# Gate/up weights laid four rows to a partition, and loaded 4 MB at a time straight into their slots from expert 18 on

## The chip, the cores and the metric

One core of one Trainium2 chip runs the whole kernel in one launch. The metric is the device time of that launch in microseconds (us). Its engines are TensorE (PE in the profile, PEld its weight loads), VectorE (DVE), ScalarE (ACT), GpSimd (POOL) and SyncE (SP), which here only waits and starts transfers; 16 DMA engines carry the transfers.

## What is computed

Two transformer blocks on 256 tokens of width 1024, all in fp32. The first is a mixing layer (stick-breaking attention and gated linear attention) with a convolutional feed-forward layer, the second pooling and latent attention with a mixture of 32 experts. The change touches the experts. Each token goes to its best 4 of 32 experts; an expert multiplies its tokens by a 1024x2048 matrix (gate and up, 8 MB) and by a 1024x1024 matrix (down, 4 MB):

```python
def expert_block(args):
    xblk, e = args
    gu = xblk @ w_gate_up[e] + b_gate_up[e]
    gate = jnp.minimum(gu[:, :D_EXPERT], SWIGLU_LIMIT)
    up = jnp.clip(gu[:, D_EXPERT:], -SWIGLU_LIMIT, SWIGLU_LIMIT)
    act = gate * jax.nn.sigmoid(SWIGLU_ALPHA * gate) * (up + 1)
    return act @ w_down[e] + b_down[e]
```

With these inputs 31 experts have at most 64 tokens, and expert 8 has 72.

## The kernel before

The first block and the attention of the second take about the first 480 us of the span. What follows is the experts, in order, as **jobs** of up to 64 tokens (`SLOTS`): one job for each expert, and a second one on the same weights for expert 8, so 33 jobs. A job is, on TensorE: `gate_up` for pairs 0 to 3 (L2432), a gather of the next job's tokens (L2428, `gather`, for the first jobs also L2415), four transposes of the activations (L2470), a bias, and `down` (L2535). The parts of the former job's result are added in between (L2492, L2502), and the job of expert 29 also makes the bias of the down matrices (L2515, `late=True`). The last job is written out apart (`last_turn`), and takes its pairs 1, 2 and 3 in halves (L2457).

**Weights.** An expert's 12 MB fill 12 slots of 8 KB in each partition: 8 for gate/up (`GU`), 4 for down (`DN`). Two neighbouring slots are a *pair* or *part* of 2 MB, and are loaded by one transfer: parts 0 to 3 are gate/up, 4 and 5 are down (`PARTS = 6`). In each partition a part takes 16 KB that are contiguous in memory, two rows of the matrix. Slots 0 to 5 are in `ring`, 6 to 11 in `ring_b`. The gather must pick the same rows of the model's width for its operand: `k_rows` steps by 2.

**Two ways into the slots.** SyncE starts all the loads, in the order of experts and parts.

- *Staged*, experts 1 to 25 (`STAGED = 26`; parts 0 and 1 of expert 1 go straight): a part goes to one of four places of 2 MB (`stage`, `stage_b`), and GpSimd copies it from there into its slots in four copies (`put_in_place`, L653), once TensorE has used what stands there. A place is filled again when its part has been copied (L422).
- *Straight*, experts 26 to 31: `next_part` waits until TensorE has used the part of the expert before (`part_used`) and loads the next one over it (L419). For expert 31, parts 1, 2, 3 and 5 come in two halves of 1 MB each (L486), with 8 KB in each partition.

TensorE waits for `in_place[part]`, which the last copy of GpSimd or the transfer itself raises. A part of an expert with two jobs is free after its second job. `gu_used` counts gate/up slots that TensorE is done with, `gu_full` is raised with the last of them, `d_used` counts down slots.

Of the kernel before, what the change touches and what calls it, by code (L numbers as in the profile page):

```python
# [32 lines left out]
P = 128  # L33
# [3 lines left out]
KT = D // P  # L37
# [13 lines left out]
E, TOPK, FE = 32, 4, 1024  # L51
# [6 lines left out]
RING = 6  # L58
CW = 2048
GU, DN = 8, 4  # L60
PAIRS = GU // 2
PARTS = PAIRS + DN // 2
PLACES = 4
STAGED = E - 6
SPLIT = 28
HI = 3

# [225 lines left out]
    return n % RING, 16 * (n // RING + 1)  # L293


def job_slot(g, slot):

    return g.t.ring[:, slot, :] if slot < RING else g.t.ring_b[:, slot - RING, :]


def pair_slot(g, pair):


    n, ring = (2 * pair, g.t.ring) if 2 * pair < RING else (2 * pair - RING, g.t.ring_b)
    return ring[:, n:n + 2, :].rearrange("p c n -> p (c n)")


def stage_place(g, place):
# [20 lines left out]
def part_used(g, job, part):  # L329

    return half_used(g, job, part, 1)
# [27 lines left out]
def sync_program(g, sp):  # L359
# [49 lines left out]
    sp.wait_ge(s.ff_o, FF_STEPS - 2)  # L409
    load_ffn(FF_STEPS - 1, "o", 0, FF_STEPS - 1)  # L410

    gate_up = w["w_gate_up_2"].rearrange("e (c p i) n -> e c p (i n)", p=P, i=2)
    down = w["w_down_2"].rearrange("e (h p i) n -> e h p (i n)", h=2, p=P)

    def part(e, k):
        return gate_up[e, k] if k < PAIRS else down[e, k - PAIRS]

    def load_part(e, k):
        sp.dma_start(pair_slot(g, k), part(e, k)).then_inc(s.in_place[k], 16)  # L419
# [19 lines left out]
        sp.dma_start(t.bias_raw[32 * q:32 * q + 32, :],  # L439
                     w["b_gate_up_2"][:, FE * (q // 2):FE * (q // 2) + FE]).then_inc(s.bias_in, 16)  # L440
    sp.dma_start(t.b_down[0:E, :], w["b_down_2"]).then_inc(s.b_down_in, 16)
    load_part(0, 3)
    load_part(0, 5)
    sp.wait_ge(*g.r2.filled("pp11"))
    load_part(0, 1)
# [1 line left out]
    load_stage(1, 3, 1)  # L447
    sp.wait_ge(s.msq_ready, NORM_AT["mla"] + 1)
    sp.wait_ge(*g.r2.filled("pa11"))
    load_part(0, 2)  # L450
    load_part(0, 4)
    load_stage(1, 4, 2)
    load_stage(1, 5, 3)
# [21 lines left out]
                load_stage(m * 2 + (q + 2), k, staged_at(q, k)[0])  # L475
    with sp.Fori(STAGED - 1, E - 2) as m:
        last = last_job(m)
        for k in range(PARTS):
            next_part(m + 1, last, k)
    last = last_job(E - 2)  # L480
    for k in range(PARTS):
# [29 lines left out]
def gpsimd_program(g, pool):  # L511
# [133 lines left out]
    def put_in_place(last, k, place, landed):  # L645

        pool.wait_ge(s.staged[place], landed)
        for i in range(2):
            pool.wait_ge(*half_used(g, last, k, i))
            pool.sem_inc(s.turn_begun, 1)  # L650
            for q in (2 * i, 2 * i + 1):
                cols = slice(D * q, D * q + D)
                ins = pool.tensor_copy(pair_slot(g, k)[:, cols], stage_place(g, place)[:, cols])  # L653
        ins.then_inc(s.in_place[k], 16)
# [4 lines left out]
    with pool.Fori(0, (STAGED - 2) // 2) as m:  # L659
        for q in range(2):  # L660
            last = last_job(m * 2 + (q + 1))
            for k in range(PARTS):
                place, landed = staged_at(q, k)
                put_in_place(last, k, place, m * 48 + 16 * landed)

    rsqrt("end2")

# [2 lines left out]
def scalar_program(g, act):  # L670
# [6 lines left out]
    def square(name, sem, value, b=0, scratch=None):  # L677
# [5 lines left out]

    act.preload_act_table_set("natural_log_exp_and_others")
    load_vectors(g, act, t.vec_b, VEC_B, s.vec_b_in)
    act.dma_start(t.vec_c[0:PAIRS, :], w["vectors"]["ffn_norm"].rearrange("a (k n) -> (a k) n", k=PAIRS)).then_inc(
        s.vec_b_in, 16)
    square("mix", s.x_in[0], 16)
    act.dma_start(t.pos_i[:], w["positions"].rearrange("(b p) -> p b", p=P),
# [352 lines left out]
def vector_program(g, dve):  # L1042
# [68 lines left out]
    for h in range(2):  # L1111
        for b in range(NB):
# [5 lines left out]
                          ALU.subtract).then_inc(s.x_split, 1)  # L1118
    split_lo(1)
    bank, done = out_of(r1, "vecb")  # L1120
    step(dve.tensor_copy(t.gain_x[:].rearrange("p (c i) -> p i c", i=2),
                         bank[:, P:P + KT].rearrange("p (i c) -> p i c", i=2)))
    dve.tensor_copy(t.vec_T[:, ROWS_A:], bank[:, 0:ROWS_B]).then_inc(done, 1)
    split_lo(2)
    split_lo(3)
# [680 lines left out]
def tensor_program(g, pe):  # L1806
# [63 lines left out]
            turn_quarter(r1, "xT", t.x_n, b, h)  # L1870
    pe.wait_ge(s.vec_b_in, 16 * (len(VEC_B) + 1))
    bank = open_bank(r1, "vecb")
    for i in range(2):
        pe.transpose(bank[:, P + PAIRS * i:P + PAIRS * i + PAIRS], t.vec_c[0:PAIRS, i:2 * P:2],
                     t.ident[0:PAIRS, 0:PAIRS])
    pe.transpose(bank[:, 0:ROWS_B], t.vec_b[0:ROWS_B, :], t.ident[0:ROWS_B, 0:ROWS_B]).then_inc(s.filled, 1)

    WHOLE = ((0, 0), (0, 1), (0, 2), (1, 0), (1, 1), (1, 2))
# [530 lines left out]
    def gather_one(f0, n):  # L2409


        for f in range(f0, f0 + n):
            k_rows = slice(2 * P * (f // 2) + f % 2, 2 * P * (f // 2) + 2 * P, 2)
            for b in range(NB):
                ins = pe.matmul(banks[6][:, (f - f0) * SLOTS:(f - f0 + 1) * SLOTS], t.h_n[:, b, k_rows],  # L2415
                                t.picks[:, b, 0:SLOTS], start=(b == 0), stop=(b == 1))
        ins.then_inc(s.gathered, 1)

    def gather(m, o):


        pe.wait_ge(s.picked, nth(m, o, 4, 2))
        pe.wait_ge(s.half_ready, nth(m, o, 1, 0))
        pe.wait_ge(s.x_parted, nth(m, o, 1, 0))
        for f in range(KT // 2):
            k_rows = slice(2 * P * (f // 2) + f % 2, 2 * P * (f // 2) + 2 * P, 2)
            for b in range(NB):
                ins = pe.matmul(banks[6][:, f * P:(f + 1) * P], t.h_half[:, b, k_rows], t.picks[:, b, :],  # L2428
                                start=(b == 0), stop=(b == 1))
        ins.then_inc(s.gathered, 1)  # L2430
# [214 lines left out]
class Semaphores:  # L2645
    def __init__(self, new):
# [136 lines left out]
class Buffers:  # L2783
# [41 lines left out]
    def vectors(self, new):  # L2825

        self.vec_a = new("vec_a", [P])
        self.vec_b = new("vec_b", [P])
        self.vec_c = new("vec_c", [2 * P])

    def mixer(self, new):

# [192 lines left out]
```

## Time and profile before

| | |
|---|---|
| median of 3 runs | 1412.66 us (1411.87 to 1412.95) |
| the profiled execution, its own time | 1416.75 us |
| its span | 1415.0 us |
| TensorE busy | 1364.8 us (96%) |
| GpSimd busy | 727.1 us (51%) |
| bytes moved | 480.81 MB, mean 340 GB/s |
| transfers from 540 us to the end of the experts | 428 GB/s but for one dip |

The span is what the profile sees; the execution's own time is 1.75 us longer, and both stand some 2 to 4 us above the median of the runs without a profile. A matmul's end is modelled, so TensorE shows as busy while it is partly waiting; waits are read from the gaps that the timeline prints in brackets, with what ended them. Each transfer's packets are shared by the 16 DMA engines.

### The profile page before, as it was taken

What the parts mean: (1) busy time and instruction counts of PE and PEld (TensorE: products, weight loads), DVE (VectorE), ACT (ScalarE), POOL (GpSimd) and SP (SyncE); (2) the same over time, 40 slices, a digit from 0 to 9 for tenths busy, and PEclk for the clock granted to TensorE, in tenths of its full rate; (3) what the DMA queues carried; (4) which work ended last, traced back from release to release, by engine and by line L of the source; (5) the groups of instructions that cost most, each with busy time, mean ns of one, the idle gap of its engine ahead of it and who ended that gap; (6) DMA issues with size and microseconds to landing.
All of it is one profiled execution on the core that took longest, in us unless ns stands there. A gap on an engine that the chain in (4) does not pass through costs nothing.

```text
span 1415.0 us, 21682 instructions
## 1 busy us (share of the span) xinstructions
PE 1364.8 (96%) x7692; PEld 778.8 (55%) x7693; DVE 754.7 (53%) x1157; ACT 304.4 (22%) x461; POOL 727.1 (51%) x723
## 2 busy tenths in 40 slices
PE   8999999999999999999999999999989999999997
PEld 8899989999976744434434334334333343334332
DVE  7675788877656546444455545444444444433322
ACT  5645453344316200000000101001000010001001
POOL 3000023322144069888869888888888888600000
PEclk9999999999999999999999999999999999999999
DMA  9444355555556889999999999999999999999996
GB/s 320 158 145 146 119 179 179 178 178 179 183 211 237 340 337 428 429 429 428 426 403 425 428 428 427 428 428 428 427 428 428 429 427 427 428 429 427 427 424 263
DMA packets 78284, 480.81 MB, mean 340 GB/s; under 512 B 7116, under 2 KB 31369, under 8 KB 53161
## 3 DMA queue, kind: packets, MB, share of 16 engines
q1 hardware_dynamic: 74910, 477.71, 83.2%
q10 hardware_dynamic: 3338, 2.62, 0.6%
q8 instruction: 24, 0.39, 0.1%
q14 instruction: 12, 0.09, 0.0%
HBM read 479.26 MB, written 1.05 MB: 339 GB/s over the span
## 4 chain that ended last, share of the span: by engine, by line
PE 54%; DMA 22%; issue 15%; POOL 5%; DVE 2%; ACT 1%; POOLq 0%; SPq 0%; DVEq 0%; ACTq 0%
DMA stage<-in_w_gate_up 14%; PE bank L2442 13%; DMA stage<-in_w_down 7%; PE bank L2130 7%; PE bank L1900 6%; PE bank L2550 6%; PE bank L2158 4%; POOL ring_b L653 3%; POOL ring L653 2%; PE bank L1850 2%; PE bank L2057 2%; PE bank L2095 2%; PE bank L1916 2%; PE bank L2428 1%; PE bank L2492 1%
## 5 line engine op out<-in xcount | busy, mean ns | idle before, releaser
L2442 PE MATMUL bank<-ring,x_T 128*64 128x512 f32 x1552 | 351.0, 598 | 22.9 <-POOL ring L653 16.8
L653 POOL COPY ring_b<-stage 128x1024 f32<-128x1024 f32 x252 | 266.8, 1102 | 45.0 <-DMA stage<-in_w_down 21.9
L2442 PEld LDWEIGHTS bank<-ring,x_T 128*64 128x64 f32 x1552 | 106.7, 137 | 246.3 <-issue 196.8
L2550 PE MATMUL bank<-ring_b,act_T 128*64 128x512 f32 x1056 | 233.9, 595 | 0.5 <-ACT act_T L999 0.5
L653 POOL COPY ring<-stage 128x1024 f32<-128x1024 f32 x192 | 198.4, 1078 | 36.7 <-DMA stage<-in_w_gate_up 24.9
L1707 DVE TENSOR_TENSOR h<-h,bank 128x512 f32<-128x512 f32 x124 | 79.6, 684 | 190.4 <-PE bank L2492 190.4
L2550 PEld LDWEIGHTS bank<-ring_b,act_T 128*64 128x64 f32 x1056 | 72.9, 137 | 144.3 <-issue 129.4
L532 POOL TENSOR_TENSOR rstd<-msq,neg_half 128x2 f32<-128x2 f32 (+2 forms) x9 | 7.7, 859 | 271.7 <-DVE msq L1066 218.0
L1683 DVE SCALAR_TENSOR_TENSOR y_lo<-bank,slot_gate,y_hi 128x512 fp32r<-128x512 f32 x33 | 24.8, 751 | 207.3 <-ACT y_hi L979 207.3
L573 POOL TENSOR_TENSOR ff_lo<-ring,ff_hi 128x2048 fp32r<-128x2048 f32 x11 | 53.0, 4820 | 145.2 <-PE bank L2130 96.5
L993 ACT ACTIVATE sig<-bias_raw 128x512 f32<-128x512 f32 x33 | 20.8, 629 | 490.8 <-DVE bias_raw L1718 490.8
L2442 PE MATMUL bank<-ring_b,x_T 128*64 128x512 f32 x512 | 116.9, 598 | 7.0 <-POOL ring_b L653 5.2
L653 POOL COPY ring<-stage_b 128x1024 f32<-128x1024 f32 x100 | 102.5, 1068 | 40.0 <-PE bank L2442 27.7
L2130 PE MATMUL bank<-h_hi,ff_hi 128*128 128x256 f32 x320 | 90.6, 283 | 0.0
L2130 PE MATMUL bank<-h_hi,ff_lo 128*128 128x256 f32 x320 | 90.6, 283 | 0.0
L2130 PE MATMUL bank<-h_lo,ff_hi 128*128 128x256 f32 x320 | 90.5, 283 | 0.0
L1101 DVE TENSOR_TENSOR ring_r<-ring,w_hi 128x2048 fp32r<-128x2048 f32 x28 | 64.1, 2295 | 27.2 <-ACT w_hi L709 27.1
L2442 PEld LDWEIGHTS bank<-ring_b,x_T 128*64 128x64 f32 x512 | 33.9, 136 | 74.4 <-issue 62.1
L979 ACT ACTIVATE y_hi<-bank,slot_gate 128x512 fp32r<-128x512 f32 x33 | 22.7, 687 | 231.9 <-PE bank L2550 231.9
L2428 PE MATMUL bank<-picks,h_half 128*128 128x128 f32 x512 | 68.1, 286 | 0.0
L858 ACT ACTIVATE ff_hi<-ring 128x2048 fp32r<-128x2048 f32 x33 | 61.6, 1905 | 28.5 <-DMA ring<-in_w_ffn_in 25.5
L2428 PEld LDWEIGHTS bank<-picks,h_half 128*128 128x128 f32 x512 | 62.8, 196 | 0.8 <-issue 0.8
(491 smaller groups left out, 2129.4 us busy)
## 6 DMA issues: line engine op xcount, KB each, us to landing
stage<-in_w_gate_up SPq DMA_DIRECT2D x73, 2048.0 KB, 15.0
stage<-in_w_down SPq DMA_DIRECT2D x38, 2048.0 KB, 15.1
stage_b<-in_w_gate_up SPq DMA_DIRECT2D x25, 2048.0 KB, 15.2
ring<-in_w_gate_up SPq DMA_DIRECT2D x21, 2048.0 KB, 23.8
ring_b<-in_w_down SPq DMA_DIRECT2D x13, 2048.0 KB, 23.0
stage_b<-in_w_down SPq DMA_DIRECT2D x12, 2048.0 KB, 15.2
ring<-in_w_in SPq DMA_DIRECT2D x22, 1024.0 KB, 5.6
ring<-in_w_ffn_in SPq DMA_DIRECT2D x22, 1024.0 KB, 6.0
```

The source lines that it names most:

```text
L573: pool.tensor_tensor(t.ff_lo[:, 1, :], t.ring[:, slot, :], t.ff_hi[:, slot, :].bitcast(F32), ALU.subtract).then_inc(s.ff_lo_pool, 1)
L653: ins = pool.tensor_copy(pair_slot(g, k)[:, cols], stage_place(g, place)[:, cols])
L858: act.activation(t.ff_hi[:, n % RING, :], t.ring[:, n % RING, :], ACT.Copy).then_inc(s.ff_hi_done, 1)
L1101: dve.tensor_tensor(t.ring_r[:, n % RING, :], t.ring[:, n % RING, :], t.w_hi[:, n % HI, :].bitcast(F32), ALU.subtract).then_inc(s.w_split, 1)
L1707: dve.tensor_tensor(t.h[:, b, cols], t.h[:, b, cols], g.banks[2 + c][:], ALU.add).then_inc(s.added, 1)
L1850: ins = pe.matmul(bank[:, 0:n], src[:, k, b * P:(b + 1) * P], wk[:, c0:c0 + n], start=(k == 0), stop=(k == len(weights) - 1))
L1900: ins = pe.matmul(into[f // 2][:, (f % 2) * T:(f % 2 + 1) * T], wt[:, k, f * P:(f + 1) * P], xt[:, 4 * half + k, :], start=((half, part) = ...
L2130: ins = pe.matmul(bank[:, f * T:(f + 1) * T], wt[:, k, f * P:(f + 1) * P], ht[:, k, :], start=(k == 0 and part == 0), stop=(k == KT - 1 an ...
L2158: ins = pe.matmul(banks[2 * b + c][:], ut[:, q, k, b * P:(b + 1) * P], wt[:, k, 512 * c:512 * c + 512], start=False, stop=last, skip_group ...
L2428: ins = pe.matmul(banks[6][:, f * P:(f + 1) * P], t.h_half[:, b, k_rows], t.picks[:, b, :], start=(b == 0), stop=(b == 1))
L2442: ins = pe.matmul(banks[n][rows, :], t.x_T[:, c, :], job_slot(g, c)[:, c0:c0 + 512], start=False, stop=(c == GU - 1), skip_group_check=True)
L2550: ins = pe.matmul(banks[4][rows, :], t.act_T[:, k, SLOTS * (c // 2):SLOTS * (c // 2) + SLOTS], job_slot(g, GU + c)[:, c0:c0 + 512], start= ...
```

## The change

Three things change together.

1. The gate/up matrix is laid out with **four** rows to a partition. Four neighbouring slots, a *quad* (4 MB), are then 32 KB of contiguous memory in each partition. A part of 2 MB is the one or the other half of that, so its 16 KB in each partition stand 32 KB apart in memory. The gather's `k_rows` steps by 4, and the gain vector `gain_x` is put in the same order (four small transposes of `vec_c` in place of two).
2. From expert 18 on (`STAGED = 18`) nothing is staged. For experts 18 to 30, `load_quad` loads parts 0 and 1 by one transfer of 4 MB, and parts 2 and 3 by another; each starts when TensorE has used both parts. Down's parts are as before. Expert 31 is loaded as before.
3. A quad raises `quad_in`; GpSimd waits for it and raises the two `in_place` that TensorE waits for. So that a quad is one piece, slots 4 to 7 are now in `ring_b`, and down's first pair is in `ring`. Of expert 0, the parts 2 and 3 change places in the order of loading.

```diff
-STAGED = E - 6
+STAGED = E - 14
...
-    n, ring = (2 * pair, g.t.ring) if 2 * pair < RING else (2 * pair - RING, g.t.ring_b)
+    ring, n = slot_home(g, 2 * pair)
...
-    gate_up = w["w_gate_up_2"].rearrange("e (c p i) n -> e c p (i n)", p=P, i=2)
+    gate_up = w["w_gate_up_2"].rearrange("e (c p i) n -> e c p (i n)", p=P, i=4)
...
     def part(e, k):
-        return gate_up[e, k] if k < PAIRS else down[e, k - PAIRS]
+        if k >= PAIRS:
+            return down[e, k - PAIRS]
+        half = 2 * CW * (k % 2)
+        return gate_up[e, k // 2][:, half:half + 2 * CW]
+
+    def load_quad(e, quad):
+        sp.dma_start(quad_slot(g, quad), gate_up[e, quad]).then_inc(s.quad_in[quad], 16)
...
     with sp.Fori(STAGED - 1, E - 2) as m:
         last = last_job(m)
-        for k in range(PARTS):
+        for quad in range(2):
+            sp.wait_ge(*part_used(g, last, 2 * quad + 1))
+            load_quad(m + 1, quad)
+        for k in range(PAIRS, PARTS):
             next_part(m + 1, last, k)
...
+    with pool.Fori(0, E - 1 - STAGED) as m:
+        for quad in range(2):
+            pool.wait_ge(s.quad_in[quad], m * 16 + 16)
+            pool.sem_inc(s.turn_begun, 1)
+            for pair in (2 * quad, 2 * quad + 1):
+                pool.sem_inc(s.in_place[pair], 16)
...
-            k_rows = slice(2 * P * (f // 2) + f % 2, 2 * P * (f // 2) + 2 * P, 2)
+            k_rows = slice(4 * P * (f // 4) + f % 4, 4 * P * (f // 4) + 4 * P, 4)
```

What SyncE has in a row in its loop over straight experts, before: a wait and a transfer of 2 MB (128x4096 fp32) for each of the four gate/up parts (down's two follow).

```order
L461 ISA
L419 ISA [waits gu_used]
L419 DMA ring<-in_w_gate_up 128x4096
L461 REGISTER_ALU
L419 ISA [waits gu_used]
L419 DMA ring<-in_w_gate_up 128x4096
L461 REGISTER_ALU
L419 ISA [waits gu_used]
L419 DMA ring<-in_w_gate_up 128x4096
L461 ISA
L419 ISA [waits gu_full]
L419 DMA ring_b<-in_w_gate_up 128x4096
```

The same place now:

```order
L500 ISA
L437 ISA [waits gu_used]
L437 DMA ring<-in_w_gate_up 128x8192
L500 ISA
L437 ISA [waits gu_full]
L437 DMA ring_b<-in_w_gate_up 128x8192
```

Two waits and two transfers are gone; the first transfer now waits for part 1 where part 0 was loaded as soon as part 0 was used, and the second for part 3.

What GpSimd has behind its staged loop, before: nothing but the last norm.

```order
L653 COPY ring_b<-stage 128x1024 [waits d_used]
L653 COPY ring_b<-stage 128x1024
L659 REGISTER_ALU
L659 COMPARE_AND_BRANCH
L532 TENSOR_TENSOR rstd<-msq,neg_half 128x2 [waits msq_ready]
```

And now (`sem_inc` prints no row of its own):

```order
L677 COPY ring_b<-stage 128x1024 [waits d_used]
L677 COPY ring_b<-stage 128x1024
L683 REGISTER_ALU
L683 COMPARE_AND_BRANCH
L689 UNCONDITIONAL_BRANCH
L689 ISA
L689 REGISTER_ALU [waits quad_in0,quad_in1]
L689 COMPARE_AND_BRANCH
L556 TENSOR_TENSOR rstd<-msq,neg_half 128x2 [waits msq_ready]
```

A loop of 13 turns has come in, which waits for each quad and passes the signal on. The staged loop above it has 8 turns in place of 12.

## Rows read from the trace of the kernel before

**Rows 1.** The page: GB/s in 40 slices of 35.4 us.

```profile
GB/s 320 158 145 146 119 179 179 178 178 179 183 211 237 340 337 428 429 429 428 426 403 425 428 428 427 428 428 428 427 428 428 429 427 427 428 429 427 427 424 263
```

**Rows 2.** Windows (busy us of each engine, then PEclk, DMA share, GB/s).

```profile
540.00:570.00 30.00, 30.00 (x160) 12.73 (x160) 18.82 (x26) 3.08 (x8) 26.78 (x26) 1.00 1.01 428
...
720.00:750.00 30.00, 30.00 (x157) 12.30 (x154) 16.04 (x24) 3.16 (x8) 19.30 (x19) 1.00 0.96 394
...
1110.00:1140.00 30.00, 27.38 (x140) 10.66 (x138) 13.23 (x21) 2.42 (x6) 25.56 (x25) 1.00 1.01 428
...
1240.00:1370.00 130.00, 122.54 (x614) 48.94 (x614) 45.54 (x100) 11.42 (x29) 0.00 (x0) 1.00 1.01 428
```

**Rows 3.** Timeline of SyncE and GpSimd around 740 us (start, us, what).

```profile
735.60 7.96 POOL L653 COPY ring<-stage 128x1024 f32<-128x1024 f32 x8 [8.91 <-PE bank L2442]
...
739.75 4.29 SPq L422 DMA_DIRECT2D stage<-in_w_down  x2
```

**Rows 4.** Timeline of TensorE, job of expert 29 (start, us, line, brackets: idle before and its end).

```profile
1316.65 3.65 PE L2442 MATMUL bank<-ring,x_T 128*64 128x512 f32 x16 [0.20 <-DMA ring<-in_w_gate_up]
...
1323.10 3.65 PE L2442 MATMUL bank<-ring,x_T 128*64 128x512 f32 x16 [0.88 <-DMA ring<-in_w_gate_up]
...
1328.40 3.65 PE L2442 MATMUL bank<-ring,x_T 128*64 128x512 f32 x16
...
1333.70 3.65 PE L2442 MATMUL bank<-ring_b,x_T 128*64 128x512 f32 x16
```

**Rows 5.** Timeline of TensorE, one row of the job of expert 28, then those of 30 and 31.

```profile
1292.16 3.65 PE L2442 MATMUL bank<-ring,x_T 128*64 128x512 f32 x16 [1.24 <-DMA ring<-in_w_gate_up]
...
1348.03 3.60 PE L2442 MATMUL bank<-ring,x_T 128*64 128x512 f32 x16
...
1352.48 3.65 PE L2442 MATMUL bank<-ring,x_T 128*64 128x512 f32 x16 [0.85 <-DMA ring<-in_w_gate_up]
...
1357.37 3.65 PE L2442 MATMUL bank<-ring,x_T 128*64 128x512 f32 x16 [0.59 <-DMA ring<-in_w_gate_up]
...
1362.27 3.65 PE L2442 MATMUL bank<-ring_b,x_T 128*64 128x512 f32 x16 [0.58 <-DMA ring_b<-in_w_gate_up]
...
1366.50 2.13 PE L2428 MATMUL bank<-picks,h_half 128*128 128x128 f32 x16
...
1369.69 7.09 PE L2550 MATMUL bank<-ring_b,act_T 128*64 128x512 f32 x32
...
1385.44 3.65 PE L2457 MATMUL bank<-ring,x_T 128*64 128x512 f32 x16
...
1389.69 1.94 PE L2457 MATMUL bank<-ring_b,x_T 128*64 128x512 f32 x8
...
1391.88 1.94 PE L2457 MATMUL bank<-ring_b,x_T 128*64 128x512 f32 x8 [0.25 <-DMA ring_b<-in_w_gate_up]
...
1393.75 0.44 PE L2479 MATMUL bank<-ident,mix_in 128*128 128x128 f32 x2
```

**Rows 6.** Timeline of SyncE: issues of the loads of expert 31.

```profile
1351.67 0.34 SPq L419 DMA_DIRECT2D ring<-in_w_gate_up  x1
...
1365.97 0.80 SPq L486 DMA_DIRECT2D ring_b<-in_w_gate_up  x2
```

**Rows 7.** Lines L2428 and L2470 (duration in ns: min/median/max).

```profile
L2428 PEld LDWEIGHTS bank<-picks,h_half x512: 194/196/198, 511.9 to 1368.2; 128*128 128x128 f32 x171
...
L2428 PE MATMUL bank<-picks,h_half x512: 281/281/385, 511.9 to 1368.3; 128*128 128x128 f32 x171
...
L2470 PEld LDWEIGHTS bank<-ident,act x132: 196/208/220, 514.3 to 1396.3; 128*128 128x128 f32 x132
...
L2470 PE MATMUL bank<-ident,act x132: 272/283/387, 514.3 to 1396.4; 128*128 128x128 f32 x132
```

**Rows 8.** The chain that ended last: a landing, and what precedes the next copy by GpSimd.

```profile
973.11 15.21 DMA stage<-in_w_down
989.84 0.69 issue
```

More of the change, by code:

```diff
@@ L293, in slot_use, with slot_home, quad_slot @@
     return n % RING, 16 * (n // RING + 1)
+def slot_home(g, slot):
+    if slot < 4 or slot in (GU, GU + 1):
+        return g.t.ring, slot if slot < 4 else slot - 4
+    return g.t.ring_b, slot - 4 if slot < GU else slot - 6
 def job_slot(g, slot):
-    return g.t.ring[:, slot, :] if slot < RING else g.t.ring_b[:, slot - RING, :]
+    ring, n = slot_home(g, slot)
+    return ring[:, n, :]
 def pair_slot(g, pair):
-    n, ring = (2 * pair, g.t.ring) if 2 * pair < RING else (2 * pair - RING, g.t.ring_b)
+    ring, n = slot_home(g, 2 * pair)
     return ring[:, n:n + 2, :].rearrange("p c n -> p (c n)")
+def quad_slot(g, quad):
+    return (g.t.ring if quad == 0 else g.t.ring_b)[:, 0:4, :].rearrange("p c n -> p (c n)")
 def stage_place(g, place):
@@ L441, in sync_program @@
     sp.dma_start(t.b_down[0:E, :], w["b_down_2"]).then_inc(s.b_down_in, 16)
-    load_part(0, 3)
+    load_part(0, 2)
     load_part(0, 5)
@@ L449, in sync_program @@
     sp.wait_ge(*g.r2.filled("pa11"))
-    load_part(0, 2)
+    load_part(0, 3)
     load_part(0, 4)
@@ L685, in scalar_program @@
     load_vectors(g, act, t.vec_b, VEC_B, s.vec_b_in)
-    act.dma_start(t.vec_c[0:PAIRS, :], w["vectors"]["ffn_norm"].rearrange("a (k n) -> (a k) n", k=PAIRS)).then_inc(
+    act.dma_start(t.vec_c[0:2, :], w["vectors"]["ffn_norm"].rearrange("a (k n) -> (a k) n", k=2)).then_inc(
         s.vec_b_in, 16)
@@ L1120, in vector_program @@
     bank, done = out_of(r1, "vecb")
-    step(dve.tensor_copy(t.gain_x[:].rearrange("p (c i) -> p i c", i=2),
-                         bank[:, P:P + KT].rearrange("p (i c) -> p i c", i=2)))
+    step(dve.tensor_copy(t.gain_x[:].rearrange("p (c i) -> p i c", i=4),
+                         bank[:, P:P + KT].rearrange("p (i c) -> p i c", i=4)))
     dve.tensor_copy(t.vec_T[:, ROWS_A:], bank[:, 0:ROWS_B]).then_inc(done, 1)
@@ L1872, in tensor_program @@
     bank = open_bank(r1, "vecb")
-    for i in range(2):
-        pe.transpose(bank[:, P + PAIRS * i:P + PAIRS * i + PAIRS], t.vec_c[0:PAIRS, i:2 * P:2],
-                     t.ident[0:PAIRS, 0:PAIRS])
+    for i in range(4):
+        pe.transpose(bank[:, P + 2 * i:P + 2 * i + 2], t.vec_c[0:2, i:4 * P:4], t.ident[0:2, 0:2])
     pe.transpose(bank[:, 0:ROWS_B], t.vec_b[0:ROWS_B, :], t.ident[0:ROWS_B, 0:ROWS_B]).then_inc(s.filled, 1)
@@ L2425, in gather @@
         for f in range(KT // 2):
-            k_rows = slice(2 * P * (f // 2) + f % 2, 2 * P * (f // 2) + 2 * P, 2)
+            k_rows = slice(4 * P * (f // 4) + f % 4, 4 * P * (f // 4) + 4 * P, 4)
             for b in range(NB):
@@ L2773, in __init__ @@
         self.half_in = {(k, i): new(f"half_in{k}{i}") for k in HALVED for i in range(2)}
+        self.quad_in = [new(f"quad_in{n}") for n in range(2)]
         self.in_place = [new(f"in_place{n}") for n in range(PARTS)]
@@ L2828, in vectors @@
         self.vec_b = new("vec_b", [P])
-        self.vec_c = new("vec_c", [2 * P])
+        new("under_sb_s", [12928])
+        self.vec_c = new("vec_c", [4 * P])
     def mixer(self, new):
```

## The prediction

> **What bounds the kernel now.** I read the page's row of GB/s first: from slice 16 on (566 us) nearly every slice stands at 427 to 429 GB/s, to the one before the last [rows 1]. So the transfers set the end of the experts. The exception is slice 20, with 403. The windows give the rest [rows 2]. At 540:570 TensorE is busy for 30.00 of 30 us and GB/s are at 428 as well; at 720:750 only at 394; later TensorE is idle (27.38 of 30 us at 1110:1140) and the transfers stay at 428, staged or straight (1240:1370).
>
> So there are three stretches. *Up to about 740 us TensorE leads.* It began with two experts' weights at hand, and expert 8's second job needs no new ones; the four places are full and the transfers run dry. GpSimd was idle for 8.91 us until TensorE had used a slot, began to copy at 735.60, and SyncE could start the next transfer at 739.75 [rows 3]. Whatever TensorE loses before this moves all that follows. *From there to 1392 us the transfers lead.* TensorE takes parts 1, 2 and 3 of expert 30 at 1352.48, 1357.37 and 1362.27, each after a wait for its transfer [rows 5]: 4.90 us to a part of 2 MB, 29.4 us to an expert, and nothing but a faster transfer shortens it. Part 1 of expert 28 was taken at 1292.16 and that of 29 at 1323.10, so there is also one slip of 1.5 us (30.94 against 29.38) [rows 4, 5]. *At the end TensorE and the transfers are close:* in the job of expert 31 it waits for part 3's second half for only 0.25 us [rows 5], and then a chain without weights follows.
>
> **The change, part by part.** The sum is made against the profiled execution (1416.75 us, span 1415.0) as a difference, and this is then put on the median, 1412.66.
>
> *Staging gone for experts 18 to 25.* Nothing, by itself: 428 GB/s staged and straight [rows 2]. GpSimd's copies go, but TensorE waits for transfers there. When SyncE turns from places to slots it needs work ahead. The first quad starts when two parts of expert 17 are used, at most 4 us for a part's copy and 7.9 us of matmuls after the first landed; the other five parts are 24.5 us of transfers, so about 12 us of them are still to come. I see no bubble.
>
> *The job with quads.* TensorE now starts pairs 0 and 1 when all 4 MB have landed, so where part 1 landed before, and pair 2 where part 3 landed. From part 3's place to the end of `down` and back it must fit in before the next quad. From [rows 5]: a pair and its combine 4.25 (1385.44 to 1389.69), pair 3 up to `down` 7.42 (1362.27 to 1369.69), `down` 7.0. Together 18.7 us, where the next expert's first quad lands 19.6 us later (four parts of 4.90). It fits, with 0.9 us to spare. Pairs 0 and 1 take 7.9 of the 9.8 us between quads. Each slot is then used up to 4.2 us later than before; what SyncE starts for expert 31, at 1351.67 (part 0) and 1365.97 (part 3) [rows 6], is taken 25 us after its start and more, so 4 us less leave the queue full. The job of expert 29, with its down bias, is longer: pair 0 and first bias 5.57 (1316.65 to 1323.10 less the wait of 0.88), then 5.30, 5.30, and 14.33 from pair 3 to the next job [rows 4, 5], 30.5 us in all. It starts expert 30 at 1353.6, 1.1 us late, and 7.9 us later, at 1361.5, TensorE is in time for part 3's place at 1362.27. So up to there the transfers still lead, and nothing is lost.
>
> *The last jobs: +3.8 us.* This is the main term. The delay has nothing behind which to hide at the end, as expert 31 needs TensorE's whole job after that of 30. Before, pair 3 of expert 30 began at 1362.27. Now pair 2 does. Then: pair 2 and combine 4.25, pair 3 up to `down` 7.42, from `down` to pair 2 of expert 31 15.75 (1369.69 to 1385.44), pair 2 and combine 4.25, pair 3 3.6. Sum 35.3: 1397.5, where pair 3 was done at 1393.75 before [rows 5]. That is +3.8. What follows is the same chain, and down's parts land no later than before.
>
> *GpSimd's hop: +0.2 us.* A quad's landing reaches TensorE through GpSimd. Below: nothing (TensorE waited on the transfer itself). Above: 0.69 us, the row between a landing and GpSimd's next copy [rows 8], which holds more instructions. It counts once, in front of the last two jobs.
>
> *Longer rows: -2.0 us.* No transfer with 32 KB to a partition is in the trace. The nearest rows are expert 31's halves, with 8 KB to a partition. From part 3 of expert 30 (1362.27) to the second half of part 3 of expert 31 (1391.88) it takes 29.61 us, with three parts in halves, and 29.38 without [rows 5]: 0.077 us for each part cut in two. A quad is two parts joined: 26 quads give 2.0 us. Between 0 (if rows are cut at 16 KB anyway) and twice it.
>
> *The gather's step of 4: +1.2 us before 740 us, +0.1 in the last jobs.* Up to the dip, 9 gathers of 16 matmuls and 48 more at the start use the strided operand, 192 in all. With step 2 a weight load takes 196 ns and a matmul 281 ns. The transposes of `act` have step 4, and 208 and 283 ns [rows 7]. The loads lie under matmuls in part, so 2 to 12 ns for each, 0.4 to 2.3 us; I take 6 ns, as a 128x128 load is about as long as the work it lies under. The Trainium skill (SBUF — State Buffer, section on the DMA port swizzle) says that SBUF lines are 16 bytes, full rate needs two hits per line, and a step of four fp32 values is where it ends. By that rule every element is now a line of its own, which speaks against the change; the 12 ns agree in sign, and if the loads doubled from 196 ns it would be up to 38 us over the 192.
>
> *Staged halves of 32 KB rows: 0.* Experts 2 to 17 now read 16 KB and skip 16 KB. Expert 31's halves read 8 and skip 8, and lost only the 0.077 us above. The bounds are -5 and +5 us (1% of the 450 us in which such parts move).
>
> *The rest: 0.* The order of parts 2 and 3 of expert 0, two more small transposes at the start.
>
> Sum: 3.8 + 0.2 - 2.0 + 1.2 + 0.1 = **+3.3 us**: 1416.0 for the median, 1420 for a profiled execution.
>
> **The rivals.** A change of 0.2% is 2.8 us, about what a measurement of this kernel can tell from none.
>
> 1. *Rows are cut at 16 KB*: no gain from quads, +5.3 us, 1418. For it: no longer row is shown. Against it: 8 KB and 16 KB differ as whole rows would.
> 2. *The joined rows save twice as much*, 4 us: +1.3, 1414. For it: a transfer fewer as well as rows fewer. Against: the halves had both, too.
> 3. *The staged reads with gaps are slower by 1%*: +4.5 on top, 1420.5. Against: the halves.
> 4. *The clock.* TensorE's longest regular wait is 1.24 us now [rows 5] with a granted clock of 1.00 [rows 2], its 2.4 GHz. In front of pair 2 the wait becomes 1.9 us. If the clock then falls to its lower level, 1.2 GHz, the next pair takes 7.2 us in place of 3.6: +3.6 in the last jobs, 1419.5. In earlier jobs it would eat its own cause.
> 5. *The other side, faster.* The quads move faster than the halves let expect. To pay for 5.3 us and another 2.8, each of 26 must save 0.31 us of its 9.79, four times my value, and the transfers would run at 442 GB/s. Then 1409 or less. Nothing in the rows speaks for it. The Trainium skill (same page, section on the DMA setup-cost knee) would: about 2 us fixed for each transfer, so make each as large as can be; by it 26 transfers fewer would save up to 52 us. Here parts follow each other every 4.90 us, with the next one under way, so the fixed part is hidden; where the queue is full I give the rule little.
>
> **How the numbers follow.** The forecast has 0.52; its own range is +1.0 to +5.0, as the gather, the hop and the slip of 1.5 us may fall, and I put 0.32 of it over +2.8 and 0.20 under. Rival 1 has 0.13, rival 2 0.14, rival 3 0.08, rival 4 0.06, rival 5 0.07. Slower: 0.32 + 0.13 + 0.08 + 0.06 = 0.59; the same: 0.20 + 0.14 = 0.34; faster 0.07. The range goes from 1411.5 (rival 2 with a free gather and no slip) to 1420.5 (rival 3), which leaves out rival 5 and the ends of 3 and 4.
>
> **What would show it.** In the profile after: parts of expert 31 and quads taken in a rhythm of 9.7 us, not 9.8; pair 2 of expert 30 starting with a wait of 0.7 to 1.9 us on GpSimd's signal or the quad; pair 3 of expert 31 without any wait, ending 35.3 us after pair 2 of expert 30 began; L2428's successor with a longer weight load; the dip at 740 us about 1 us later. The forecast is wrong if TensorE still waits for part 3 of expert 31, if a slice at 428 falls, or if the experts' transfers run dry near 990 us.

## The result: 1449.3 us against 1412.8, 2.5% slower

The changed kernel took 1449.3 us (median of 4 runs, 1447.09 to 1451.24), the kernel before beside it 1412.81 us (1411.87 to 1416.81). The ratio is 1.025 with an interval of 1.0236 to 1.0264: 36.5 us more, where the forecast was 3.3 more and the range ended at 1420.5. The prediction was wrong, in size and in place. One execution of experiment 3, at 1721.62 us and a mean granted clock of 0.75, where its others have 0.997 or 0.998, is left out of that experiment's ratio.

The page of the changed kernel: its span, TensorE's and GpSimd's busy time, and GB/s in 40 slices of 36.2 us.

```profile
span 1448.0 us, 21340 instructions
...
PE 1422.9 (98%) x7694; PEld 843.9 (58%) x7695; DVE 730.2 (50%) x1157; ACT 304.4 (21%) x461; POOL 522.0 (36%) x531
...
GB/s 314 174 147 125 135 190 156 198 195 165 217 150 309 276 317 429 428 428 429 428 280 372 430 428 428 429 428 383 405 427 429 429 437 427 430 428 435 426 423 201
```

The spans differ by 33.0 us and not by 36.5, because the profiled execution of the kernel before was itself 4 us above its median. TensorE is busy for 58 us more than it was. The row of GB/s has two holes: 280 and 372 from 724 to 796 us, where before there was the one slice of 403 near 740 [rows 1], and 383 and 405 from 977 us on, where before there was none. Everywhere else from slice 16 to the one before the last they stand at 423 or more. So nothing is wrong with the transfers' rate. They stood still twice, and what let them stand still is to be looked for on TensorE.

The lines of the gather (L2457, before L2428) and of the transposes of `act` (L2499, before L2470), as in [rows 7]: duration in ns, min/median/max.

```profile
L2457 PEld LDWEIGHTS bank<-picks,h_half x512: 309/330/332, 518.6 to 1401.5; 128*128 128x128 f32 x171
L2457 PE MATMUL bank<-picks,h_half x512: 396/397/500, 518.6 to 1401.6; 128*128 128x128 f32 x171
...
L2499 PEld LDWEIGHTS bank<-ident,act x132: 194/208/302, 522.2 to 1429.2; 128*128 128x128 f32 x132
L2499 PE MATMUL bank<-ident,act x132: 272/283/387, 522.4 to 1429.4; 128*128 128x128 f32 x132
```

A weight load of the gather takes 330 ns where it took 196, a matmul 397 where it took 281. The transposes, with the same step of 4, stand at 208 and 283 as ever. The timeline of TensorE shows what this is in time that nobody else can use:

```profile
546.65 3.97 PE L2457 MATMUL bank<-picks,h_half 128*128 128x128 f32 x16
550.46 0.63 PE L2499 MATMUL bank<-ident,act 128*128 128x128 f32 x4
```

Sixteen matmuls now hold the engine for 3.81 us (546.65 to 550.46). Before, the row of 2.13 us [rows 5] was followed by the transposes after 1.96 us:

```profile
1366.50 2.13 PE L2428 MATMUL bank<-picks,h_half 128*128 128x128 f32 x16
1368.46 0.63 PE L2470 MATMUL bank<-ident,act 128*128 128x128 f32 x4
```

That is 1.85 us more for each gather, 0.116 us for each matmul, where the sum of the prediction had 0.006. Every job does a gather, and up to the first hole TensorE leads.

The first hole, GpSimd and SyncE of the changed kernel, as in [rows 3]:

```profile
757.03 8.05 POOL L677 COPY ring<-stage 128x1024 f32<-128x1024 f32 x8 [23.24 <-PE bank L2471]
...
761.29 4.29 SPq L443 DMA_DIRECT2D stage<-in_w_down  x2
```

GpSimd waits 23.24 us for TensorE (before 8.91) and begins to copy at 757.03 (before 735.60). The dip is 21.4 us later, not "about 1". It accounts for 21.4 of the 33.0 us. The other 11.6 us come after it, and here are the windows of that stretch (columns as in [rows 2]) and TensorE's waits for a quad in all of it:

```profile
960.00:1020.00 60.00, 60.00 (x290) 26.06 (x288) 22.18 (x44) 4.84 (x12) 47.02 (x46) 1.00 0.91 384
...
1140.00:1200.00 60.00, 60.00 (x290) 26.23 (x291) 19.74 (x46) 5.50 (x14) 0.00 (x0) 1.00 1.00 428
1200.00:1260.00 60.00, 58.01 (x280) 25.45 (x278) 18.16 (x42) 4.84 (x12) 0.00 (x0) 1.00 1.00 429
```

```profile
PE bank L2471 <- POOLq L694: 5.3, 5, 1.1
```

TensorE is never idle up to 1200 us. Before, it was waiting for transfers already at 1110:1140 (27.38 of 30 us) [rows 2]. Then five waits for quads follow, 5.3 us together, the first of them ending at 1212.40. So what bounds the kernel has changed from 760 to about 1210 us: there TensorE with its longer job leads, and the transfers set the pace only for the last experts.

### The profile page after: what moved, and what is told of

Same layout as the page of the kernel before. It is cut to its first block, busy times and chain, and to the rows that moved or that the text cites. A ratio compares the mean times of both kernels' runs of the same rounds, so it can differ in the third digit from the quotient of the medians.

```text
span 1448.0 us, 21340 instructions
## 1 busy us (share of the span) xinstructions
PE 1422.9 (98%) x7694; PEld 843.9 (58%) x7695; DVE 730.2 (50%) x1157; ACT 304.4 (21%) x461; POOL 522.0 (36%) x531
## 4 chain that ended last, share of the span: by engine, by line
PE 84%; DMA 9%; issue 4%; DVE 2%; ACT 0%; POOLq 0%; SPq 0%; DVEq 0%
PE bank L2471 28%; PE bank L2579 12%; DMA ring_b<-in_w_gate_up 9%; PE bank L2159 7%; PE bank L2457 7%; PE bank L1929 6%; PE bank L2187 4%; PE bank L2521 3%; PE bank L1880 2%; PE bank L2086 2%; PE bank L2124 2%; PE bank L1945 2%; PE bank L2292 1%; PE bank L2245 1%; PE bank L2499 1%
## 5 line engine op out<-in xcount | busy, mean ns | idle before, releaser
L2471 PE MATMUL bank<-ring_b,x_T 128*64 128x512 f32 x1024 | 235.2, 602 | 5.3 <-POOLq L694 5.3
L2471 PE MATMUL bank<-ring,x_T 128*64 128x512 f32 x1040 | 232.3, 599 | 0.0
L677 POOL COPY ring_b<-stage 128x1024 f32<-128x1024 f32 x168 | 179.8, 1112 | 21.7 <-DMA stage<-in_w_gate_up 9.0
L677 POOL COPY ring<-stage 128x1024 f32<-128x1024 f32 x132 | 132.4, 1047 | 51.2 <-PE bank L2471 25.0
L2457 PE MATMUL bank<-picks,h_half 128*128 128x128 f32 x512 | 127.2, 402 | 0.0
L2457 PEld LDWEIGHTS bank<-picks,h_half 128*128 128x128 f32 x512 | 121.9, 329 | 0.8 <-issue 0.8
L2579 PE MATMUL bank<-ring,act_T 128*64 128x512 f32 x528 | 120.6, 599 | 0.5 <-ACT act_T L1029 0.5
L2579 PE MATMUL bank<-ring_b,act_T 128*64 128x512 f32 x528 | 118.9, 592 | 0.0
L2579 PEld LDWEIGHTS bank<-ring_b,act_T 128*64 128x64 f32 x528 | 38.0, 137 | 75.3 <-issue 75.3
L2579 PEld LDWEIGHTS bank<-ring,act_T 128*64 128x64 f32 x528 | 35.0, 137 | 68.8 <-issue 56.9
```

The costliest lines, as they stand in the source:

```text
L2471: ins = pe.matmul(banks[n][rows, :], t.x_T[:, c, :], job_slot(g, c)[:, c0:c0 + 512], start=False, stop=(c == GU - 1), skip_group_check=True)
L2579: ins = pe.matmul(banks[4][rows, :], t.act_T[:, k, SLOTS * (c // 2):SLOTS * (c // 2) + SLOTS], job_slot(g, GU + c)[:, c0:c0 + 512], start= ...
```

## The experiments

**1. The gather's step alone.** The kernel before, with one thing changed:

```diff
-k_rows = slice(2 * P * (f // 2) + f % 2, 2 * P * (f // 2) + 2 * P, 2)
+k_rows = slice(4 * P * (f // 4) + f % 4, 4 * P * (f // 4) + 4 * P, 4)
```

> The kernel before with one edit: the gather's operand is read with a step of 4 instead of 2 (it then picks other rows than the reference, the work is the same). Theory A, the step itself doubles a gather's matmul from 118 to 235 ns: about 21.4 us more up to the dip near 740 us, as in the changed kernel (735.60 against 757.03), then the transfers lead at 29.4 us to an expert against a job of 28.05, and the last gather adds 1.9: about 1436 us, and the dip with GpSimd's long wait at about 757. Theory B, the quads and the early end of the staging cost the most: within 5 us of 1413. Theory C, the reads with gaps in memory are what is slow: 1413.

Measured: 1442.98 us against 1413.8, ratio 1.0206 (1.019 to 1.0222), 29.2 us more. No transfer was touched, and the time is most of the way to the changed kernel's. Its gather, its hole and its transfers late in the kernel:

```profile
L2428 PEld LDWEIGHTS bank<-picks,h_half x512: 308/330/332, 517.7 to 1395.0; 128*128 128x128 f32 x171
```

```profile
756.18 4.10 POOL L653 COPY ring<-stage 128x1024 f32<-128x1024 f32 x4 [23.24 <-PE bank L2442]
```

```profile
1260.00:1320.00 60.00, 60.00 (x290) 26.14 (x288) 20.25 (x51) 4.85 (x12) 0.00 (x0) 1.00 1.01 428
```

The step of four, alone, makes the same weight load and the same wait of 23.24 us. My expectation of 1436 was some 7 us short. I had let the transfers take the lead again after the hole, but TensorE is busy for 60.00 of 60 us at 1260:1320 and waits for no transfer after 760 us. At 428 GB/s an expert takes 29.4 us and a job of TensorE now takes 28.05 (its gathers start at 1163.82 and 1191.87 in the changed kernel), so the transfers gain only on TensorE's stock, 1.35 us a job, and the experts run out first.

**2. The rest alone.** The changed kernel with the gather's step back at 2, on layout, staging and quads as changed:

```diff
-k_rows = slice(4 * P * (f // 4) + f % 4, 4 * P * (f // 4) + 4 * P, 4)
+k_rows = slice(2 * P * (f // 2) + f % 2, 2 * P * (f // 2) + 2 * P, 2)
```

> The changed kernel with one edit: the gather's step is 2 again (it then picks rows that do not match the layout of the weights). Theory A: only the rest of the forecast is left, +3.8 for the last jobs, +0.2 for the hop, -2.0 for the longer rows: about 1414.9 us, between 1412.5 and 1418. Theory B: 1430 or more. Theory C: some part of the 36 us stays, a rate below 425 GB/s in the staged stretch.

Measured: 1415.42 us (11 runs), ratio 1.0015 (1.0006 to 1.0025), by the ratio 2.1 us more than before. The forecast without its terms for the gather was +2.0. Its last jobs, as in [rows 5]:

```profile
1357.13 3.65 PE L2471 MATMUL bank<-ring_b,x_T 128*64 128x512 f32 x16 [1.54 <-POOLq L694]
...
1365.60 2.13 PE L2457 MATMUL bank<-picks,h_half 128*128 128x128 f32 x16
...
1388.80 3.65 PE L2486 MATMUL bank<-ring_b,x_T 128*64 128x512 f32 x16
1392.38 0.44 PE L2508 MATMUL bank<-ident,mix_in 128*128 128x128 f32 x2
```

Pair 2 of expert 30 starts after a wait of 1.54 us, pair 3 of expert 31 starts with none, and it is done 35.25 us after pair 2 began (1357.13 to 1392.38); the prediction had 35.3. From the end of pair 3 of expert 31 back, this part stands as it was forecast. Only the distance can be compared and not the place: GpSimd's copies after the first hole began at 732.58 in this execution and at 735.60 in the one of the kernel before.

The trace also shows rival 4 at work. At 1297.26 TensorE comes out of a wait of 1.97 us, and its pair takes 5.32 us in place of 3.65:

```profile
1297.26 5.32 PE L2471 MATMUL bank<-ring_b,x_T 128*64 128x512 f32 x16 [1.97 <-POOLq L694]
```

```profile
1295.30:1297.26 1.96, 0.00 (x1) 0.00 (x1) 1.29 (x2) 0.00 (x0) 0.00 (x0) 0.99 0.94 401
1297.26:1300.60 3.34, 3.34 (x8) 0.99 (x10) 0.00 (x0) 0.00 (x0) 0.00 (x0) 0.50 1.00 427
1300.60:1304.00 3.40, 3.40 (x18) 1.06 (x16) 0.72 (x2) 0.00 (x0) 0.00 (x0) 0.99 1.02 434
```

The granted clock is 0.50, the lower level of 1.2 GHz, for 3.3 us behind the wait, and 0.99 again after that. Such falls stand behind five of the seven waits of 1.96 to 1.98 us in this trace (at 1034.21, 1121.89, 1180.35, 1238.82 and 1297.26). Behind the other two, at 1004.97 and 1092.66, the pair took its 3.65:

```profile
1004.97 3.65 PE L2471 MATMUL bank<-ring_b,x_T 128*64 128x512 f32 x16 [1.96 <-POOLq L694]
```

A fall costs 1.7 us there and nothing in the end: from 1034.21 to 1297.26 these pairs start every 29.23 us whether the clock fell or not, since TensorE waits for the next quads anyway. After the 1.54 us at 1357.13, the only such wait that had no slack behind it, the pair took its 3.65.

**3. The earlier end of staging alone.** The kernel before with:

```diff
-STAGED = E - 6
+STAGED = E - 14
```

> The kernel before with one edit: staging ends at expert 17, the rest goes straight in parts of 2 MB; layout and gather as before. My forecast priced this at nothing: 1412.8 within 1 us, no dip in GB/s near 990 us. The rival: the smaller stock of weights costs, a dip near 990 us and 3 to 8 us more.

Measured: 1413.02 us (11 runs), ratio 0.9994 (0.9985 to 1.0004). Nothing, as priced.

**4. Layout and order without quads.** The changed kernel's layout of four and gather of four, all parts of 2 MB, staging up to expert 25 as before (GpSimd's loop for the quads goes too):

```diff
-STAGED = E - 14
+STAGED = E - 6
...
-        for quad in range(2):
-            sp.wait_ge(*part_used(g, last, 2 * quad + 1))
-            load_quad(m + 1, quad)
-        for k in range(PAIRS, PARTS):
+        for k in range(PARTS):
```

> The changed layout alone (four rows to a partition, parts of 2 MB read with gaps, gather with step 4), staging up to expert 25 and no quads. Theory A: the same as the gather alone, about 1436 us within 2 us, 428 GB/s wherever the queue is full. Theory C: clearly over 1440 us and a rate below 425 GB/s. Theory B: near 1413.

Measured: 1442.29 us, ratio 1.0206 (1.0191 to 1.0222), the same as for the gather alone; the expected 1436 is missed for the same reason as in experiment 1. At 1110:1300, with the gate/up parts read as 16 KB and 16 KB skipped, the transfers move 428 GB/s:

```profile
1110.00:1300.00 190.00, 190.00 (x908) 81.66 (x910) 77.68 (x144) 15.84 (x39) 119.63 (x115) 1.00 1.01 428
```

Rival 3, the slower reads with gaps, falls.

**5. The operand in one piece.** If the step is the cause, the cure is to write `h_n` in the order in which the gather reads it. ScalarE, which writes it, does that with the same two instructions:

```diff
-        act.activation(t.h_n[:, b, :], t.h[:, b, :], ACT.Copy,
+        act.activation(t.h_n[:, b, :].rearrange("p (c i q) -> p c q i", i=4, q=P),
+                       t.h[:, b, :].rearrange("p (c q i) -> p c q i", i=4, q=P), ACT.Copy,
...
-            k_rows = slice(4 * P * (f // 4) + f % 4, 4 * P * (f // 4) + 4 * P, 4)
+            k_rows = slice(P * f, P * f + P)
```

> The changed kernel, with the normalised rows h_n written once in the order in which the gather reads them, so that its operand is contiguous; the result is the reference's. Theory A (line of 16 bytes: the cost is the step of the operand, and nothing else of the change is dear): about 1414 us, as with step 2 (1415.4) less 6 ns for each of the 192 matmuls before the dip; a gather's matmul every 111 to 118 ns, not 235. Theory B or C would leave 1420 or more.

Measured: 1415.12 us (12 runs), ratio 1.0009 (1.0 to 1.0019), with all three parts of the change in it. The gather's loads fall below those of step 2:

```profile
L2458 PEld LDWEIGHTS bank<-picks,h_half x512: 186/192/192, 510.1 to 1367.3; 128*128 128x128 f32 x171
L2458 PE MATMUL bank<-picks,h_half x512: 275/275/377, 510.1 to 1367.4; 128*128 128x128 f32 x171
```

34 of the 36.5 us are gone with this one edit. It isn't free on ScalarE: each of the two instructions takes 2076 ns, where the changed kernel has 1148. In kernel 5:

```profile
L996 ACT ACTIVATE x_n<-h,rstd x2: 2060/2076/2091, 478.4 to 480.2; 128x1024 f32<-128x1024 f32 x2
```

That is 1.9 us more on an engine that has time: the first gather starts at 484.98 in place of 484.79 us.

**6 and 7. The tail in parts.** Kernel 5, with expert 30 (then experts 29 and 30) loaded in parts of 2 MB again, so that the last jobs don't wait for a whole quad:

```diff
-    with sp.Fori(STAGED - 1, E - 2) as m:
+    with sp.Fori(STAGED - 1, E - 3) as m:
...
+    last = last_job(E - 3)
+    for k in range(PARTS):
+        next_part(E - 2, last, k)
```

GpSimd's loop ends one turn earlier as well (two for the second kernel).

> As fixed, but expert 30 is loaded in parts of 2 MB like expert 31; quads for 18 to 29 only. If the 3.8 us at the end come from expert 30's quads alone, and the longer rows do save 0.08 us a quad (24 of them, 1.9 us): about 1410 us, 1.5 to 3 us under the kernel before. If the late start of the jobs costs elsewhere, or if the rows save nothing: 1412 to 1414.

> As fixed_tail, but expert 29, whose job is longer by the down bias, is loaded in parts too; quads for 18 to 28 only; the result is the reference's. In fixed_tail the job of expert 29 began 30.6 us before that of expert 30, and TensorE never waited after it. If this is what kept fixed_tail (1412.2) from 1410: 1410 to 1411. If the quads' savings are smaller than thought or given back by the clock: 1412.

Measured: 1412.18 us (12 runs), ratio 0.9991 (0.9983 to 1.0), and for the second (expert 29 in parts too) 1411.4 us (11 runs), ratio 0.999 (0.9981 to 0.9999). Taking expert 30 out of the quads gives back 2.9 us, where the prediction's term for the last jobs was 3.8 + 0.2, less 0.15 for two quads. With expert 29 out as well TensorE waits for no weights in the last 100 us. Both are the fastest kernels of this study, 1.2 and 1.4 us below the kernel before, within what a measurement of it can tell from nothing. The 1410 that I hoped for from the first is not reached, and the second lies between the two values that I had given it, so these two runs don't decide between their theories.

**8. The same cure without the change.** The kernel before, `h_n` written in its gather's order (the edit of experiment 5 with `i=2`).

> The kernel before with h_n written in the gather's order, the operand contiguous instead of step 2; the result is the reference's. Contiguous weight loads of the trace follow each other in about 111 ns against 118, so 1.3 us less before the dip: 1412 against 1413.5. If a step of 2 costs nothing (two values to a line of 16 bytes are enough): no change.

Measured: 1412.56 us (11 runs), ratio 0.9993 (0.9985 to 1.0002). The interval holds 1: the step of 2 was almost free, so there is little to win, and 0.9 us of it can't be told from nothing.

**9. A transfer of 4 MB in rows of 16 KB.** Quads with the old layout of two: two pieces of 16 KB in each partition, the same waits and the same hop.

```diff
+    quads = w["w_gate_up_2"].rearrange("e (q c p i) n -> e q p c (i n)", c=2, p=P, i=2)
...
+        sp.dma_start(quad_slot(g, quad).rearrange("p (c n) -> p c n", c=2), quads[e, quad])
```

> The old layout (two rows to a partition, gather with step 2), but experts 18 to 30 in transfers of 4 MB whose rows are 16 KB: quads without longer rows; the result is the reference's. If the 0.08 us come from the number of rows: quads land every 9.79 us and the time is 2 us over the changed kernel with step 2, about 1417. If they come from the number of transfers: 9.72 us and 1415.

Measured: 1418.17 us (7 runs), ratio 1.0032 (1.0021 to 1.0043). It is 2.8 us over kernel 2, or 2.4 by the two ratios, and their intervals touch. The gathers of TensorE, which the transfers pace, show why. The kernel with rows of 16 KB, then kernel 2 with rows of 32 KB, then the kernel before, each over two jobs:

```profile
1103.98 2.13 PE L2458 MATMUL bank<-picks,h_half 128*128 128x128 f32 x16
...
1162.74 2.13 PE L2458 MATMUL bank<-picks,h_half 128*128 128x128 f32 x16
```

```profile
1101.13 2.13 PE L2457 MATMUL bank<-picks,h_half 128*128 128x128 f32 x16
...
1159.60 2.13 PE L2457 MATMUL bank<-picks,h_half 128*128 128x128 f32 x16
```

```profile
1104.64 2.13 PE L2428 MATMUL bank<-picks,h_half 128*128 128x128 f32 x16
...
1163.45 2.13 PE L2428 MATMUL bank<-picks,h_half 128*128 128x128 f32 x16
```

That is 58.76 us for two experts with 16 KB in 4 MB, 58.47 with 32 KB in 4 MB, 58.81 with 16 KB in 2 MB. The last kernel still stages there; kernel 3, which loads the same parts of 2 MB straight, has 58.78 between the same two gathers (1097.52 and 1156.30). One transfer in place of two saves nothing that shows; half as many rows save 0.17 us an expert (58.81 less 58.47, halved), 0.085 for each quad, or 0.078 against kernel 3. The prediction had 0.077.

**10. How the step costs.** The kernel before, with step 8 in the 48 matmuls of the first gathers and step 3 in the others:

```diff
-            k_rows = slice(2 * P * (f // 2) + f % 2, 2 * P * (f // 2) + 2 * P, 2)
+            k_rows = slice(f, D, 8)
...
-            k_rows = slice(2 * P * (f // 2) + f % 2, 2 * P * (f // 2) + 2 * P, 2)
+            k_rows = slice(f, f + 3 * P, 3)
```

> The kernel before, with the operand of the first gather (48 matmuls) read with a step of 8 and that of the jobs' gathers with a step of 3 (both pick other rows than the reference; the work is the same). Theory A, two of four fp32 values of a 16-byte line must be used for the full rate: step 8 is as step 4, 235 ns, and step 3 (12 bytes, a new line nearly every time) lies between 118 and 235, near 235 if every element that opens a line alone pays. Its rival, a cost that grows with the distance: step 8 well over 235 ns, step 3 about 175.

Measured: 1427.69 us against 1415.32, one execution of each. Step 3 in its place in a job, and step 8 in the first gather:

```profile
624.22 3.04 PE L2428 MATMUL bank<-picks,h_half 128*128 128x128 f32 x16
...
484.45 7.78 PE L2415 MATMUL bank<-picks,x_n 128*128 128x64 f32 x32
```

Sixteen matmuls take 2.03 us in one piece (kernel 5), 2.13 with step 2, 3.04 with step 3, 3.97 with step 4. The first gather's 32 take 3.88 us with step 2, 7.62 with step 4, 7.78 with step 8, and a load there 329 ns with step 4 and 335 with step 8. Step 8 decides against a cost that grows with the distance: from step 4 on it stops growing but for 2%. Step 3 decides nothing, as its 180 ns for a matmul (3.04 us less one matmul of 339 ns, over 15) lie near the rival's 175 and within what theory A allowed.

In units of 16 bytes, the steps 1, 2, 3, 4 and 8 touch 1/4, 1/2, 3/4, 1 and 1 unit for each value. Up to a half the cost is small, and from there 3/4 and 1 stand as 3.04 to 3.97. This is the rule of the Trainium skill (SBUF — State Buffer, section on the DMA port swizzle), two hits to a 16-byte line for full rate, and the trace agrees with it at each of the five steps. The same note of the Trainium skill would still let four fp32 values be free; here three already cost half as much again.

At step 4 the granted clock doesn't set the pace either. In the changed kernel it falls to 0.50 in the middle of the first gather (484.79 to 492.34), and here are three microseconds of its matmuls and loads at each level (busy, count; then PEclk, DMA share, GB/s):

```profile
485.00:488.00 3.00, 3.00 (x14) 3.00 (x14) 1.00 1.01 431
...
489.20:492.20 3.00, 3.00 (x14) 3.00 (x13) 0.50 1.02 437
```

**11. The gather of four with the shorter staging, and no quads.** The one line of experiment 1 with that of experiment 3.

> The kernel before with the gather's step of 4 (it picks other rows than the reference, the work is the same) and staging only up to expert 17, then parts of 2 MB straight. With step 2 this end of the staging cost nothing. Theory: with the slow gather TensorE leads all the way, the transfers are ahead by all the stock there is, and must stop while the stock shrinks from 20 to 12 MB, so they run dry near 990 us as in the changed kernel and are missed later: 3 to 7 us over the gather alone (1443.0), 1446 to 1450, and most of what the changed kernel has over it. Rival: the 6 us are those of the quads; then 1443 within 1 us.

Measured: 1442.96 us (5 runs), ratio 1.0212 (1.0199 to 1.0226). A miss: I expected 3 to 7 us over experiment 1, and it can't be told from it. The smaller stock alone costs nothing that shows in the time. What it does in the trace is in the waits of TensorE for weights after 900 us, of this kernel:

```profile
PE bank L2442 <- DMA ring<-in_w_gate_up: 0.6, 1, 0.6
PE bank L2442 <- DMA ring_b<-in_w_gate_up: 0.6, 1, 0.6
```

Two waits, 1.2 us together, where the changed kernel has five and 5.3 us. To compare the rest of the way, here is the gather of the same job and then the last gather in this kernel, in that of experiment 1, and in the changed one:

```profile
1193.06 3.97 PE L2428 MATMUL bank<-picks,h_half 128*128 128x128 f32 x16
...
1395.04 3.98 PE L2428 MATMUL bank<-picks,h_half 128*128 128x128 f32 x16
```

```profile
1191.02 3.97 PE L2428 MATMUL bank<-picks,h_half 128*128 128x128 f32 x16
...
1391.56 3.97 PE L2428 MATMUL bank<-picks,h_half 128*128 128x128 f32 x16
```

```profile
1191.87 3.98 PE L2457 MATMUL bank<-picks,h_half 128*128 128x128 f32 x16
...
1398.07 3.97 PE L2457 MATMUL bank<-picks,h_half 128*128 128x128 f32 x16
```

It takes 201.98 us, 200.54 and 206.20. The changed kernel loses 5.66 us over the gather's step alone, all of it behind 1191.87, and 4.22 us of that over the same staging without quads. 4.22 is close to the time of one pair with its combine, 4.25 in the prediction.

## Why the prediction was wrong, point by point

**The gather's step of 4 is the step that failed.** It stood at +1.2 us, with bounds of 2 to 12 ns for a matmul; it measured 116 ns. The sum took its price from the transposes of `act`, which have the same step and 208 ns a load, as the nearest row. But 12 ns is a transpose with step 4 less a gather with step 2, so two kinds of instruction are mixed in it. The trace of the kernel before has transposes of the same shape whose operand is in one piece:

```profile
L2479 PEld LDWEIGHTS bank<-ident,mix_in x66: 137/140/143, 501.9 to 1393.8; 128*128 128x128 f32 x66
...
L1828 PEld LDWEIGHTS bank<-ident,h x48: 138/140/223, 193.8 to 477.6; 128*128 128x128 f32 x48
```

Like against like, step 4 takes such a load from 140 to 208 ns, 68 ns more, and the row that the prediction took as reassuring shows the cost. It hardly reaches the time there: eight transposes in one piece follow each other every 110 to 114 ns (L1828; a group's time less that of its last matmul), four with step 4 every 116. The gather's matmuls went from one every 123 ns to one every 238. Why a transpose hides its longer load and a gather doesn't is open. No row before showed a 128x128 weight load of a gather with step 4, so the 12 ns were not an upper bound at all. The upper bound was in the sentence next to it, on the rule of the Trainium skill (SBUF — State Buffer, section on the DMA port swizzle): loads doubled from 196 ns, "up to 38 us over the 192". They became 330 ns, and the 192 matmuls before the hole cost 22 us, 21.4 of which reach it. I weighed that rule against a difference of two rows that don't compare, and let it decide.

**What TensorE loses behind the hole.** The prediction let the transfers lead from the hole to 1392 us, whatever happened at the hole. With a job of 28.05 us in place of 26.2 this no longer holds. From the start of GpSimd's copies to the end of the span it took 679.4 us before (735.60 to 1415.0), 685.2 with the gather alone (756.18 to 1441.4), 691.0 in the changed kernel (757.03 to 1448.0). So of 33.0 us 21.4 lie before the hole, 5.8 are TensorE's own lead to the end, and 5.8 come with quads and the shorter staging.

**These last 5.8 us** fit the term for the last jobs, met earlier. With quads a job needs pair 1 where it needed pair 0, and pair 3 where pair 2, so it catches up with the transfers sooner; it does so in the window 1200:1260, and without quads (experiment 11) only at the wait that ends at 1325.64:

```profile
1325.64 3.65 PE L2442 MATMUL bank<-ring,x_T 128*64 128x512 f32 x16 [0.58 <-DMA ring<-in_w_gate_up]
```
From there the transfers pace TensorE at 29.2 us a job in place of 28.05. The five waits show the place and the three spans the size. That the other 1.4 us are from the smaller stock is only argued, from the two waits of experiment 11; in its time it doesn't show. And the quads were run with the slow gather only together with the smaller stock, so how much of the 4.22 us the quads would cost without it is open.

**The rest of the sum held.** *The last jobs, +3.8:* 35.25 us measured for the 35.3 worked out, and 2.9 us came back when expert 30 went in parts. *Longer rows, -2.0:* 0.078 to 0.085 us a quad, 2.0 to 2.2 us in all, and by the rows and not the number of transfers (experiment 9). *Staging, reads with gaps:* nothing, in experiments 3 and 4. *The hop, +0.2:* 0.17 us in the chain of kernel 2, from a quad's landing at 1209.41 (1190.13 and 19.28) to TensorE's start, with GpSimd's signal in between:

```profile
1190.13 19.28 DMA ring_b<-in_w_gate_up
...
1209.58 3.65 PE bank L2471 x16
```

Together kernel 2 is 2.1 us over the kernel before; the forecast less the gather was 2.0. With terms of 0.1 to 4 us and an interval of 1.3 us, this near a hit of the sum is partly luck; the single terms are what was measured.

**The bubble near 990 us.** I saw none, and with the fast gather there is none. The changed kernel has one, for the reason of the first hole: TensorE is late with every slot. SyncE starts nothing from 991.09 to 1014.68:

```profile
991.09 5.72 SPq L443 DMA_DIRECT2D stage<-in_w_down  x2
1014.68 0.34 SPq L437 DMA_DIRECT2D ring<-in_w_gate_up  x1
```

TensorE had work for another 190 us and didn't wait. But the transfers move 295 GB/s at 1000:1020, which puts them back by some 6 us of their time, and TensorE catches up with them that much sooner behind 1200 us. In experiment 11 the same stretch has 351 and then 399 GB/s, some 5 us, and little came of it. The dry stretch was named among the signs that would make the forecast wrong, and it came as a result of the error, not as its cause.

**The rivals.** Of rival 1, rows cut at 16 KB, and rival 2, twice the saving, neither came: 0.078 to 0.085 lies beside 0.077. Rival 3 fell. Rival 4's clock falls do occur, where there is slack, and cost 1.7 us each in place of the 3.6 that it had, as the clock comes back within the pair. Rival 5 went by a fixed cost for each transfer (the Trainium skill, SBUF — State Buffer, section on the DMA setup-cost knee); with the queue full 58.76 us against 58.81 show none, as the prediction had argued.

## What to carry to other kernels

When a layout of weights is changed, look first at what the matmuls that feed it now read, and how far apart: the step of an operand in its 128x128 weight load was worth some ten times what all of the rest of the forecast came to (34 us against 2 to 4). Price an operation from the same instruction with the same kind of operands, and a step from two rows that differ in nothing else. Where no such row exists let the rule set the end of the range, not a row that is merely near. And where the order of reading changes, let the engine that writes the data write it in that order; here it cost ScalarE 1.9 us and the kernel 0.2, and brought 34 us back.

## What the hardware showed that I had not expected

A step between values costs the weight loads of a gather next to nothing up to two fp32 values, half as much again at three, and nearly double at four and eight (2.13, 3.04, 3.97 us for sixteen, 2.03 in one piece). At step 4 they go at the same pace with the clock at 1.00 and at 0.50. A transpose's load grows as well, from 140 to 208 ns, but its pace hardly changes.

TensorE fell to half its clock for 3.3 us behind five of seven waits of 1.96 to 1.98 us between full bursts (experiment 2), and not behind the other two, nor those of 1.54 us there or of 1.24 us before [rows 5].

Rows of 32 KB still move faster than rows of 16 KB, by 0.8 to 0.9% (0.078 to 0.085 of 9.80 us), where a doubled transfer with the same rows gains nothing that shows.

ScalarE takes 2076 ns to write 128x1024 fp32 in the gather's order of four, and 1148 ns in the plain order (experiment 5); in the gather's order of two it takes 2090 (experiment 8).
